# Constant float32 products put into TensorE's waits around the router and at the border of two layers

## The reference

```python
for l in range(DEPTH):
    mix = hybrid_mixer(x, w_in[l], ...)
    x = layer_norm(ALPHA * x + mix, ln1_g[l], ln1_b[l])
    ffn = grouped_moe(x, router_w, router_bias, w_gate[l], w_up[l], w_down[l])
    x = layer_norm(ALPHA * x + ffn, ln2_g[l], ln2_b[l])
```

```python
scores = jax.nn.sigmoid((t @ router_w).astype(jnp.float32))
...
a = jnp.einsum('td,edf->etf', t, w_gate)
u = jnp.einsum('td,edf->etf', t, w_up)
hidden = jax.nn.silu(a) * u * gates.T.astype(t.dtype)[..., None]
out = jnp.einsum('etf,efd->td', hidden, w_down)
```

## Time and profile before

| | |
|---|---|
| Median of 3 runs | 2092.38 us (2089.34 to 2094.97) |
| The profiled execution | 2092.66 us |
| Its span | 2090.5 us, so 2.2 us lie around it |
| TensorE matmul busy | 1953.0 us, 93% |
| TensorE weight load busy | 1128.3 us, 54% |
| VectorE busy | 652.7 us, 31% |
| ScalarE busy | 342.4 us, 16% |
| HBM read | 535.73 MB, 257 GB/s over the span |
| Chain that ended last | PE 62%, DMA 31%, DVE 5% |

### The profile page before, as it was taken

How to read it: one execution, slowest core, us unless ns; L and a number is a source line. 1 busy time by engine, 2 the same in 40 slices (tenths; PEclk the granted TensorE clock), 3 DMA queues, 4 the chain that set the end, 5 groups by cost and what they waited for, 6 DMA issues and landing times.

```text
span 2090.5 us, 26749 instructions
## 1 busy us (share of the span) xinstructions
PE 1953.0 (93%) x10877; PEld 1128.3 (54%) x10877; DVE 652.7 (31%) x1287; ACT 342.4 (16%) x622; POOL 16.8 (1%) x106
## 2 busy tenths in 40 slices
PE   8999999899799999999899999998997999999995
PEld 4688865564544344444347888565645444334442
DVE  1225544441611111111332536545324111111015
ACT  0103220100311011111211132201104111101112
POOL 3000000000000000000000000000000000000000
PEclk9999999999899999999999999999998999999998
DMA  7444342106599999999945433421246999999995
GB/s 234 140 140 142 101 142 100 61 22 221 201 393 422 422 422 422 422 422 422 388 129 164 137 121 124 139 82 61 77 168 260 422 422 422 422 422 422 422 422 237
DMA packets 128831, 539.00 MB, mean 258 GB/s; under 512 B 15856, under 2 KB 20464, under 8 KB 78320
## 3 DMA queue, kind: packets, MB, share of 16 engines
q1 hardware_dynamic: 128752, 537.86, 66.0%
HBM read 535.73 MB, written 2.10 MB: 257 GB/s over the span
## 4 chain that ended last, share of the span: by engine, by line
PE 62%; DMA 31%; DVE 5%; issue 1%; ACT 1%; SPq 1%; DVEq 0%
PE bank L717 19%; PE bank L706 16%; DMA x_t<-in_w_down_dram 16%; DMA x_t<-in_w_up_dram 15%; PE bank L1127 7%; PE bank L1164 4%; PE bank L954 3%; PE bank L741 3%; PE bank L1083 2%; PE bank L652 1%; PE bank L827 1%; PE bank L931 1%; PE bank L842 1%; SPq L579 0%; PE bank L925 0%
## 5 line engine op out<-in xcount | busy, mean ns | idle before, releaser
L706 PE MATMUL bank<-x_t,ring 128*128 128x256 f32 x1536 | 346.2, 384 | 0.0
L706 PEld LDWEIGHTS bank<-x_t,ring 128*128 128x128 f32 x1536 | 291.4, 192 | 50.3 <-issue 11.9
L717 PE MATMUL bank<-ring,x_t 128*128 128x512 f32 (+1 forms) x640 | 258.4, 557 | 1.9 <-DMA ring<-in_w_in_dram 1.9
L1127 PE MATMUL bank<-ring,prob_t 128*64 128x512 f32 x768 | 173.7, 595 | 31.8 <-DMA ring<-in_w_up_dram 31.7
L1937 DVE TENSOR_TENSOR region_a<-bank,region_a 128x512 f32<-128x512 f32 x16 | 11.1, 692 | 580.7 <-PE bank L1127 580.7
L717 PEld LDWEIGHTS bank<-ring,x_t 128*128 128x128 f32 x640 | 120.2, 192 | 116.5 <-issue 109.6
L717 PE MATMUL bank<-ring,mix_acc 128*128 128x512 f32 x384 | 178.4, 602 | 1.5 <-ACT mix_acc L1350 1.5
L1127 PEld LDWEIGHTS bank<-ring,prob_t 128*64 128x64 f32 x768 | 58.1, 137 | 144.0 <-issue 144.0
L1083 PEld LDWEIGHTS bank<-prob_t,x_nat 128*128 128x128 f32 x1024 | 120.7, 199 | 14.4 <-issue 11.4
L1083 PE MATMUL bank<-prob_t,x_nat 128*128 128x128 f32 x1024 | 123.8, 284 | 2.8 <-DVE prob_t L1871 2.8
L1127 PE MATMUL bank<-ring,region_a 128*64 128x512 f32 x512 | 113.4, 595 | 0.0
(11 more groups left out here) (364 smaller groups left out, 1936.0 us busy)
## 6 DMA issues: line engine op xcount, KB each, us to landing
ring<-in_w_gate_dram SPq DMA_DIRECT2D x96, 1024.0 KB, 21.5
ring<-in_w_in_dram SPq DMA_DIRECT2D x80, 1024.0 KB, 5.0
ring<-in_w_up_dram SPq DMA_DIRECT2D x64, 1024.0 KB, 19.1
region_b<-in_w_down_dram SPq DMA_DIRECT2D x48, 1024.0 KB, 21.9
ring<-in_w_out_dram SPq DMA_DIRECT2D x32, 1024.0 KB, 5.1
region_b<-in_w_gate_dram SPq DMA_DIRECT2D x32, 1024.0 KB, 21.1
x_t<-in_w_up_dram SPq DMA_DIRECT2D x32, 1024.0 KB, 23.5
ring<-in_w_down_dram SPq DMA_DIRECT2D x32, 1024.0 KB, 20.6
```

Of the source, the lines that this page charges most:

```text
L706: m = pe.matmul(b[c // 2][:, (c % 2) * T:(c % 2 + 1) * T], w[:, kk, c * P:(c + 1) * P], xT[:, k, :], start=(k == 0 and c % 2 == 0), stop=( ...
L717: m = pe.matmul(b[t][:, 0:width], lhs[:, k, t * P:(t + 1) * P], w[:, kk, 0:width], start=(k == 0), stop=(k == KC - 1))
L1127: m = pe.matmul(bank[2 + w][rows, :], xg_half[k // 8][:, k % 8 * P + rows.start:k % 8 * P + rows.stop], exp_slot[(n + e) % EXP_SLOTS][:, k ...
```

## The change

A helper spin(b, n) issues n products of the identity and win_mask into bank b, which nobody reads at that time. It is called at seven places. The last scatter of a layer is split in two calls, pieces 0 to 5 and pieces 6 and 7; in layer 0 there are ten products between them. In all 42 products are added in layer 0 and 32 in layer 1. No wait is added or removed.

```diff
+            def spin(b, n):
+
+                for _ in range(n):
+                    pe.matmul(bank[b][:, 0:3 * P], ident[:, :], win_mask[:, :], start=True, stop=True)
+
...
                         turn_x(g, 1, bank[XT_BANKS[1][g]])
+                    spin(5, 2 if t else 6)
                     pe.wait_ge(xt_act.sem, xt_act.at(l, 8 + 2 * t))
...
                     m.then_inc(part_done.sem, 1)
+                    if t == 0:
+                        spin(5, 3)
...
                 m.then_inc(logit_done.sem, 1)
 
+                spin(6, 13)
                 pe.wait_ge(member_ready.sem, member_ready.at(l, 1))
...
+                spin(6, 4)
                 pe.wait_ge(pick2_ready.sem, pairs0 + (l + 1))
                 gather()
...
                 pair_turn(last_pair, True)
 
+                spin(2, 4)
                 pe.wait_ge(scat_ready.sem, pairs1 + (l + 1))
                 pe.wait_ge(y_ready.sem, (pairs1 + (l + 1)) * 4)
-                scatter(pairs1)
+                scatter(pairs1, range(6))
+                if l < depth - 1:
+                    spin(2, 10)
+                scatter(pairs1, [6, 7])
```

## The result

The changed kernel takes 2098.45 us (median of 11 runs) against 2091.74 us for the kernel before (11 runs): a ratio of 1.0030, 95% interval 1.0022 to 1.0038, so slower by 4.6 to 7.9 us. One of the 11 runs after took 2314.46 us at a mean clock of 0.845; it is left out of the ratio. The forecast was +4.15 us, 2096.5, with a chance of 0.67 on a change within 0.3%; the measured +6.7 us sits on that line, and which side it falls on was a near thing.

A forecast was written before the change was run, and what follows sets the result against it. TensorE's waits and low clock bound the router and border, DMA the expert stage. Terms 1.6 + 0.2 + 1.6 + 0.75 = +4.15 us gave about 2096.5 us; its own range 2094.7 to 2100, overall range 2090 to 2102.

The forecast's parts named there:

- The clock, held: Router stages and layer border: added products keep TensorE's granted clock at 1.00 where it fell to about one half.
- The second rival: Clock falls despite the products, placed at the thirteen before the ranks: +9.8 us in all, 2102 us, chance 0.12.
- The price of a product: All seven places: one added float32 product is two MATMULs, 0.64 us at the upper clock, 1.28 at the lower.
- The first rival: Everything fits: an added product costs 0.32 us, each group just under its wait; -9.8 us, 2083 us, chance 0.10.
- Router stage, +1.6 us a layer: Up to the first expert product: overruns 0.6, 3.6 and 1.15 us, less 1.0 at ranks and 2.75 at gather.
- The gather: Router stage, 64 MATMULs before the first expert product: 7.2 us at full clock instead of 9.94, so -2.75 us.
- The ranks: Router stage: five rank products run closer together at full clock, 0.23 us spacing instead of 0.43, so -1.0 us.
- Border, +0.2 us: Between the layers: +0.2 us in all, including 0.75 us overrun before the scatter.
- tile 0's chain: Layer border: transposes start later but run at full clock; panel 0's first eight k steps end +0.2 us later.
- The cover: Layer border: tile 1's LayerNorm is 2.9 us late, but TensorE turns to tile 1 later still, 0.7 us to spare.
- Tail, +0.75 us: Layer 1, four products before the last scatter on the chain ending the kernel, already at full clock: +0.75 us.
- The restart of the stream: Expert stage, DMA-bound: a later first expert product delays the weight stream's restart and the layer's end by as much.

The follow-up runs named there:

- half-width kernel: Changed kernel with all its counts, each added product reading 192 mask columns instead of 384: 2082.31 us, ratio 0.9952 to the kernel before.
- the fitted: Changed kernel with counts cut to 3, 1, 1, 7, 2, 2 and 5 products: 2082.76 us, ratio 0.9960 to the kernel before.
- the border-only: Changed kernel without the router stage's products, keeping four before each last scatter and ten between the layers: 2093.03 us, ratio 1.0007 to the kernel before.
- the twenty-six: Changed kernel with 26 products before the ranks instead of thirteen: 2114.34 us, ratio 1.0109 to the kernel before.
- ranks-and-gather: Kernel before plus seven products before the ranks and two before the gather, none elsewhere: 2082.56 us, ratio 0.9959 to the kernel before.
- the seven: Changed kernel with seven products before the ranks instead of thirteen, all else kept: 2090.45 us, ratio 0.9995 to the kernel before.
- ranks-only: Kernel before plus seven products before the ranks, none elsewhere: 2084.92 us, ratio 0.9974 to the kernel before.

## Why the prediction was right, and where its sizes were off

**The clock, held.** Right: 1.00 in every stretch named. The second rival, that the clock falls all the same, is out: it reads 1.00 among 7, 13 and 26 products.

**The price of a product.** 0.64 us was taken, 0.65 measured within a group (8.47 us for thirteen), and 0.66 to 0.69 in the groups of six, three and two, from the first product to the next instruction's start. The five groups of the router stage together take 18.5 us where 17.9 was forecast. The price of 0.325 us for two MATMULs that the Trainium skill's "Back-to-back issue gap" would give ("TensorE: Matmul & The Clock Gate") is out for float32: the half-width kernel cost that much, the change twice as much. The first rival's arithmetic was right, though. Where the products do fit, the kernel takes 2082 to 2083 us, and 2083 was its figure.

**Router stage, +1.6 us a layer:** +1.96 and +2.00. Its terms in layer 0, with the shift of 1.13 us that was there before the stage taken off: router product of tile 1 at +1.08 (0.6 forecast), ranks at +4.70 (4.2), gather at +4.66 (4.35), first expert product at +1.96 (1.6). The term that was mis-sized is the sum of the products' lengths, by 0.6 us. The gather gave back 2.70 us where 2.75 was forecast (7.24 us, 7.2 taken). The ranks gave back more than forecast, 1.3 us for 1.0: the five take 1.03 us (565.50 to 566.53) and took 2.32 before (559.67 to the wait before the gather).

**Border, +0.2 us:** +0.89. The 0.75 us before the scatter was exact. The step that failed is the one after it, tile 0's chain. From the scatter's first product to tile 0's transposes it is 10.43 us (1037.62 to 1048.05) instead of 10.1, and panel 0 then waits 0.38 us for ScalarE's copies (L722), which the forecast had ready in time. The cover held for tile 1, by 1.3 us.

**Tail, +0.75 us:** 0.75, and 0.2 more, at the first two products of the last scatter. The change, then before:

```profile
2072.69 0.69 PE L1104 MATMUL bank<-y_hi,scat_rows 128*128 128x512 f32 x1
2073.22 0.39 PE L1106 MATMUL bank<-y_lo,scat_rows 128*128 128x512 f32 x1
```

```profile
2065.42 0.50 PE L1095 MATMUL bank<-y_hi,scat_rows 128*128 128x512 f32 x1 [1.56 <-DVE y_lo L1946]
2065.76 0.39 PE L1097 MATMUL bank<-y_lo,scat_rows 128*128 128x512 f32 x1
```

Directly behind added products the first one starts 0.53 us ahead of the next; behind a wait it is 0.34. The trace shows it in all four profiles with the four products there (the stage is 25.3 us) and in no other (25.1 us). It may be the end of the added products themselves: at the border the last of their MATMULs, which stand 0.32 us apart, starts only 0.03 us ahead of the scatter's. The forecast counted neither. In the profile of the change the last piece, at 2079.81 us, also runs at the lower clock, before it did not (2072.35 us), but from its start to the end it is 18.2 us in both.

**The restart of the stream.** Right, one for one: the expert stages measure 454.8 to 455.4 us in every profile but that of before in layer 1 (456.03), with first products that lie 17 us apart.

**The sum.** +4.15 forecast, 5.8 us in the touched stages, 6.7 by the medians. The remaining 1 us or so of the medians is not explained by any step. What the single profiles have beyond it is for the most part the clock, in places that nothing edits. The stretch from the DeltaNet's first transposes to the last panel is 143.0 us in the profiles of before, the fitted, the border-only, the twenty-six, the half-width and the ranks-and-gather kernels and 144.1 in those of the change, the seven and the ranks-only kernels. Over 400 to 420 us the clock is 0.91 to 0.93 in the six and 0.83 to 0.85 in the three; before and the change:

```profile
400.00:420.00 20.00, 15.80 (x112) 11.25 (x113) 11.00 (x24) 3.11 (x4) 0.00 (x0) 0.91 0.02 9
```

```profile
400.00:420.00 20.00, 16.75 (x92) 11.88 (x92) 9.92 (x22) 3.14 (x4) 0.00 (x0) 0.83 0.03 11
```

The start takes 19.3 to 22.2 us. Its sixteen 512-column MATMULs, in before and in the change:

```profile
12.23 8.94 PE L717 MATMUL bank<-ring,x_t 128*128 128x512 f32 x16 [1.94 <-DMA ring<-in_w_in_dram]
```

```profile
12.24 10.09 PE L722 MATMUL bank<-ring,x_t 128*128 128x512 f32 x16 [2.19 <-DMA ring<-in_w_in_dram]
```

They stand 0.85 us apart at first and 0.43 us later; in the kernel of ranks and gather, with 19.3 us, they are 0.43 us apart almost from the first. None of this follows the edits, so a single profile differs by one or two us for reasons that lie outside the change. Whether the medians hold a part that its code causes stays open.

**The rule for the lower clock.** The Trainium skill's "Terms" section ("TensorE: Matmul & The Clock Gate") charges half of the throttled time, 16.5 us for the stretches named. With the clock at 1.00 in all of them and nothing overrun the kernel gained 9.0 us. The measurement decides: of time at the lower clock only that part comes back in which TensorE was working and others waited for it.

## What to carry to other kernels

Before filling a wait of TensorE to hold its clock, read from the trace what one filler costs in the kernel's own type (here a float32 product is two MATMULs and takes 0.65 us at 384 columns), and add no more than fits: the fitted fill was worth 9 us, the same fill at twice its length cost 6.7. Fill the long wait ahead of the longest matmul work first; here seven products before the ranks and two before the gather carried nearly all of it. And ask what starts when the filled stretch ends: a stream that restarts there passes every overrun on to the end, unshortened.

## What was not expected of the hardware

Half the filler held the clock as well as all of it, and a product of an identity with a mask of two values did so like any other. The short fall at 549 us is absent from one profile whose code there is that of before, and one kernel's nine runs have mean clocks of 0.982 to 0.989: with waits of 1 to 2.3 us whether the clock falls differs from execution to execution. A wait of 2.8 us in the mixer, after which the clock reads 0.66 over five us, was worth more to fill (1.6 and 2.6 us by the stages of the two layers, 4.8 by the medians) than all the waits of the border and of tile 1 (some 2 us by the stages).
